# Second layer: output projection, norm before the experts and router logits in one program, tile by tile

## The reference, cut to what matters

```python
def finish(o):                                  # inside diff_mixer
    o = rms_norm(o, p['subln'], SUBLN_EPS) * (1.0 - lambda_init)   # per head of 128 columns
    return o.reshape(*o.shape[:2], C_HEADS * 2 * HEAD_DIM) @ p['w_out']
...
x = x + mods_l[2] * out_l
hl = modulate(rms_norm(x), mods_l[3], mods_l[4])        # x * rstd * (1 + scale) + shift
...
grp_logits = hf @ w_grp.astype(f32) + b_grp.astype(f32)         # moe_ffn, 4 groups
exp_logits = (hf @ w_rt.astype(f32) + b_rt.astype(f32)).reshape(n, N_GROUPS, EXPERTS_PER_GROUP)
```

## Time and profile before

| what | us |
|---|---|
| median of three runs | 4664.04 |
| span of the profiled execution | 4663.1 |
| first DMA of the output projection to its first product | 3585.46 to 3631.87 |
| products of the output projection to the last one | to 3762.4 |
| rest of that phase, and the norm | to 3812.1 |
| the router's logits | to 3833.1 |
| the rest of the routing | to 3890.5 |
| experts and most of the combination | to 4640 |

### The profile page before, as it was taken

How to read it: one execution, slowest core, us unless ns; L and a number is a source line. 1 busy time by engine, 2 the same in 40 slices (tenths; PEclk the granted TensorE clock), 3 DMA queues, 4 the chain that set the end, 5 groups by cost and what they waited for, 6 DMA issues and landing times. The chain is left out here.

```text
span 4663.1 us, 88181 instructions
## 1 busy us (share of the span) xinstructions
PE 3727.8 (80%) x34186; PEld 2390.1 (51%) x34187; DVE 1882.9 (40%) x4414; ACT 1372.4 (29%) x3096; POOL 592.2 (13%) x926
## 2 busy tenths in 40 slices
PE   4998995698898685599999539989996654999973
PEld 1886553688888673133333128876664531333321
DVE  3322555677777563300000264327775332000004
ACT  2212664366664212011111021116665120111111
POOL 0000000144444220200000202100000102000001
PEclk7999997899999897699999759989998867999986
DMA  7221001122222245968899852240001234589995
GB/s 301 76 84 69 10 10 47 42 72 74 78 69 77 83 149 197 302 253 309 307 389 392 333 195 93 77 157 11 11 10 64 79 115 190 199 323 369 407 427 218
DMA packets 254657, 777.07 MB, mean 167 GB/s; under 512 B 77972, under 2 KB 166568, under 8 KB 223624
## 3 DMA queue, kind: packets, MB, share of 16 engines
q1 hardware_dynamic: 201064, 641.55, 36.9%
q10 hardware_dynamic: 38736, 82.33, 4.6%
q0 software_dynamic: 14544, 48.79, 2.7%
HBM read 647.12 MB, written 117.60 MB: 164 GB/s over the span
## 5 line engine op out<-in xcount | busy, mean ns | idle before, releaser
L3076 PE MATMUL ex_bY<-ex_w,ex_aT 128*64 x880 | 389.1, 595 | 73.5 <-DVE ex_aT L3139 73.5
L3076 PE MATMUL ex_bG<-ex_w,ex_xT 128*64 x880 | 403.9, 614 | 39.6 <-SPq L2997 25.8
L3079 PE MATMUL ex_bG<-ex_w,ex_xT 128*64 128x512 f32 x880 | 403.9, 614 | 0.0
L3079 PE MATMUL ex_bY<-ex_w,ex_aT 128*64 128x512 f32 x880 | 389.4, 595 | 0.0
L3076 PE MATMUL ex_bU<-ex_w,ex_xT 128*64 x880 | 386.6, 592 | 0.0
L3079 PE MATMUL ex_bU<-ex_w,ex_xT 128*64 128x512 f32 x880 | 386.6, 592 | 0.0
L3137 DVE TENSOR_TENSOR ex_a<-ex_sg,ex_bU 128x512 f32<-128x512 f32 x55 | 37.9, 689 | 812.4 <-PE ex_bU L3079 812.4
L3076 PEld LDWEIGHTS ex_bG<-ex_w,ex_xT 128*64 128x64 f32 x880 | 123.8, 142 | 301.7 <-issue 301.7
L3076 PEld LDWEIGHTS ex_bY<-ex_w,ex_aT 128*64 128x64 f32 x880 | 116.0, 137 | 299.7 <-issue 299.7
L1036 DVE TENSOR_SCALAR_CACHE_REDUCE ad_p<-ad_S 128x512 f32<-128x512 f32 (+1 forms) x384 | 215.7, 600 | 101.5 <-PE ad_S L946 101.5
L3076 PEld LDWEIGHTS ex_bU<-ex_w,ex_xT 128*64 128x64 f32 x880 | 120.6, 137 | 247.4 <-issue 247.4
(11 more groups left out here) (450 smaller groups left out, 8544.0 us busy)
## 6 DMA issues: line engine op xcount, KB each, us to landing
ex_w<-in_moe_w_gate SPq DMA_DIRECT2D x64, 2048.0 KB, 11.9
ex_w<-in_moe_w_up SPq DMA_DIRECT2D x64, 2048.0 KB, 16.2
ex_w<-in_moe_w_down SPq DMA_DIRECT2D x64, 2048.0 KB, 15.3
yb_dram<-ex_y ACTq DMA_DIRECT2D x55, 512.0 KB
rt_mw<-in_mod_w SPq DMA_DIRECT2D x24, 1024.0 KB, 7.6
n_mw<-in_mod_w SPq DMA_DIRECT2D x16, 1024.0 KB, 8.2
kb_dram<-rs_pout SPq DMA_DIRECT2D x60, 256.0 KB, 2.8
rs_KB<-kb_dram SPq DMA_DIRECT2D x120, 128.0 KB, 2.6
```

The costliest lines, as they stand in the source:

```text
L3076: nc.tensor.matmul(bank[0:BR, :], stationary[:, k, 0:BR], w[:, ds(slot0 + (offset + k * n), 512)], start=k == 0, stop=k == tiles - 1)
L3079: m = nc.tensor.matmul(bank[BR:P, :], stationary[:, k, BR:P], w[:, at:at + 512], start=k == 0, stop=k == tiles - 1)
```

## The change

`odd_outproj_phase` takes the place of `outproj_phase` and of the second layer's `norm_phase`, and it makes the logits too. `outproj_phase` and its loop over pairs are gone; the new streams are written out for 8 tiles.

- The inner norm's factor times (1 - lambda_init) is now a column of 128 values, one for each row of a weight strip. ACT and DVE put it into the weights while they split them (L2741, L2794). POOL's multiplication of `o` is gone.
- Four buffers for weight strips, and separate buffers `sq` for the squares. PE's first block of products takes strip k as soon as it is split (`w_rest`, k + 1). Only one gate row is loaded.
- A class `RowNorm` holds the next norm and the logits of a tile: ACT squares and takes the root, DVE scales, POOL adds the shift row, SP stores `h`, PE turns the tile through one bank, ACT copies it, PE multiplies (the turned rows stationary, the 36 router columns moving) and DVE adds the bias into `L`, which stays in SBUF. PE does this for tile q - 2 while it makes the products of tile q.
- `route_phase` with `L` given loads neither weights nor biases and begins with the choice of the group.

In the diff, the four loops inside `odd_outproj_phase` are those of SP, PE, ACT and DVE, in this order; the last two stand behind the split of the weights.

```diff
-def outproj_phase(nc, sems, tag, d, layer, o_dram, w_dram, src, dst, first=0, subln=None):
+class RowNorm:
...
+    def load(self, sp, cond):
...
+        for t, which in ((self.shift_row, SHIFT2), (self.scale_row, SCALE2)):
+            sp.dma_start(t[:, :], row_of(d["mods"][l, cond, which * D:(which + 1) * D])).then_inc(self.const_in, 16)
...
+    def prepare(self, dve):
+        self.nc.vector.memset(self.eps[:, :], RMS_EPS).then_inc(self.eps_set, 1)
+        dve.wait_ge(self.const_in, 16 * 6)
+        self.nc.vector.tensor_scalar(self.scale_row[:, :], self.scale_row[:, :], 1.0, None, ALU.add).then_inc(self.ready, 1)
...
+    def shift(self, pool, q):
...
+        self.scaled.wait(pool, q)
+        self.shifted.did(self.nc.gpsimd.tensor_tensor(self.h[:, u, :], self.h[:, u, :], self.shift_row[:, :], ALU.add))
...
+    def turn(self, pe, q, b):
+        u = q % 2
+        if b == 0:
+            self.shifted.wait(pe, q)
+        if q or b:
+            self.lifted.wait(pe, q if b else q - 1, 0 if b else 1)
+        for k in range(4):
+            z = self.nc.tensor.transpose(self.bankH[:, k * P:(k + 1) * P], self.h[:, u, (4 * b + k) * P:(4 * b + k + 1) * P], self.ident[:, :])
...
+    def logits(self, pe, q):
...
+        self.lifted.wait(pe, q)
+        if q:
+            self.taken.wait(pe, q - 1)
+        for k in range(KT):
+            z = self.nc.tensor.matmul(self.bankL[:, 0:TD], self.hT[:, u, k, :], self.wr[:, k, :], start=k == 0, stop=k == KT - 1)
...
+def odd_outproj_phase(nc, sems, d, o_dram, src, dst, h_dram, L):
...
+                for q in range(T):
+                    if q + 4 < T:
+                        load_o(q + 4)
+                    store_x(q)
+                    if q + 2 < T:
+                        load_x(q + 2)
+                    norm.store(sp, q, row(q))
...
+                turn(0)
+                turn(1)
+                for q in range(T + 2):
                     for b in US:
+                        if q < T:
+                            products(q, b)
+                        if q >= 2:
+                            norm.turn(pe, q - 2, b)
+                    if q + 2 < T:
+                        turn(q + 2)
+                    if q >= 2:
+                        norm.logits(pe, q - 2)
...
+                for q in range(T + 2):
+                    if q >= 2:
+                        for b in US:
+                            norm.lift(act, q - 2, b)
+                    if q + 2 < T:
+                        lead(q + 2)
+                    if q + 3 < T:
+                        square(q + 3)
+                    if q < T:
+                        norm.square(act, q)
+                        norm.root(act, q)
+                    if q + 3 < T:
+                        root(q + 3)
...
+                norm.prepare(dve)
+                total(2)
+                unit(2)
+                for q in range(T + 2):
+                    if q < T:
+                        result(q)
+                    if q + 2 < T:
+                        rest(q + 2)
+                    if q + 3 < T:
+                        total(q + 3)
+                    if q < T:
+                        norm.scale(dve, q)
+                    if q >= 2:
+                        norm.take(dve, q - 2)
+                    if q + 3 < T:
+                        unit(q + 3)
...
-def route_phase(nc, sems, tag, d, layer, hT, first, slot_dram, slots, gates, tok, table, sil=None):
+def route_phase(nc, sems, tag, d, layer, hT, first, slot_dram, slots, gates, tok, table, sil=None, L=None):
...
-    outproj_phase(nc, sems, "o1", d, 1, o, d["od_w_out"][0], x2, x3, CT, d["od_subln"][0])
-    moe(1, x3, out, CT, d["final_gain"])
+    with ExitStack() as ctx:
+        L = static(ctx, "L1", [P, NT - CT, TD])
+        odd_outproj_phase(nc, sems, d, o, x2, x3, h, L)
+        moe(1, x3, out, CT, d["final_gain"], L=L)
```

More of the change, by code:

```diff
@@ L2517, in outproj_phase @@
-        rounds = (NT - first) // 2
+        row = lambda q: (CT + q) * P
         with nc.Block() as block:
@@ L2570, in _, with turn @@
+            @block.gpsimd
+            def _(pool):
+                for q in range(T):
+                    norm.shift(pool, q)
             @block.tensor
             def _(pe):
-                pe.wait_ge(c_in, 16 * nc_in)
-                def turn(m, u):
-                    if pre:
-                        po.wait(pe, f"sub{u}", m)
-                    else:
-                        pe.wait_ge(o_in[u], 16 * m + 16)
+                pe.wait_ge(ident_in, 16)
+                def turn(q):
+                    normed.wait(pe, q)
@@ L2600, in body @@
[L2600 to L2616 removed]
+                            z = nc.tensor.transpose(tr[b][:, k * P:(k + 1) * P], o[:, q % 2, (4 * b + k) * P:(4 * b + k + 1) * P], ident[:, :])
@@ new lines, in turn, with products @@
+                        turned.did(z)
+                def products(q, b):
+                    u = q % 2
+                    if b == 0:
+                        rested.wait(pe, q)
+                    if q >= 2:
+                        gated.wait(pe, q - 2, b)
+                    for k in range(KT):
+                        if q == 0 and b == 0:
+                            pe.wait_ge(w_rest, k + 1)
+                        for n, (p, r) in enumerate(((oh, wh), (oh, wl), (ol, wh))):
+                            z = nc.tensor.matmul(acc[u][b][:, :], p[:, u, k, :], r[:, k, b * 512:(b + 1) * 512], start=k == 0 and n == 0, stop=k == KT - 1 and n == 2)
+                    multiplied.did(z)
@@ L2644, in _, with square, root @@
-                pair_loop(act, first, body)
+                act.wait_ge(eps_set, 1)
+                def square(q):
+                    act.wait_ge(o_in[q % 2], 16 * (q // 2 + 1))
+                    if q >= 2:
+                        summed.wait(act, q - 2)
+                    squared.did(nc.scalar.activation(sq[:, q % 2, :], o[:, q % 2, :], ACT.Square))
+                def root(q):
+                    summed.wait(act, q)
+                    if q >= 2:
+                        inverted.wait(act, q - 2)
+                    rooted.did(nc.scalar.activation(sd[:, q % 2, :], ss[:, q % 2, :], ACT.Sqrt, scale=1.0 / P, bias=eps[:, 0:1]))
@@ new lines, in result @@
+                def result(q):
+                    u = q % 2
+                    if q == 0:
+                        dve.wait_ge(gate_in, 16)
+                    for b in US:
+                        multiplied.wait(dve, q, b)
+                        gated.did(nc.vector.tensor_tensor(t[:, u, b * 512:(b + 1) * 512], acc[u][b][:, :], gate[:, b * 512:(b + 1) * 512], ALU.mult))
+                    dve.wait_ge(x_in[u], 16 * (q // 2 + 1))
+                    for b in US:
+                        gated.wait(dve, q, b)
+                        x_done.did(nc.vector.tensor_tensor(x[:, u, b * 512:(b + 1) * 512], t[:, u, b * 512:(b + 1) * 512], x[:, u, b * 512:(b + 1) * 512], ALU.add))
```

372 lines of the change are left out of this document (207 added, 165 removed).

## The result

| | before | changed |
|---|---|---|
| median, first comparison | 4666.09 us (4 runs) | 4584.07 us (4 runs, 4582.33 to 4590.16) |
| ratio, 95% interval | | 0.9823 [0.9811, 0.9834] |
| median, second comparison | 4671.97 us (9 runs) | 4589.61 us (5 runs, 4578.53 to 4591.02) |
| ratio, 95% interval | | 0.9819 [0.9805, 0.9832] |
| span of the profiled execution | 4663.1 | 4580.5 |

The change saves 82 us of the whole. The forecast was 4567 with a range from 4554 to 4598: the mechanism held, and the gain was put 17 us too high. 8.3 us of these lie in the forecast stretch (150.8 forecast, 159.1 measured). 6.0 us lie in code that is the same in both kernels: the first load of `o` stands 4.5 us later than in the trace of before (3590.00 against 3585.46), and the part behind the stretch is 1.5 us longer.

The account below looks back on a forecast made before the run. TensorE was taken as idle in a 247.7 us stretch, waiting for strips, GpSimd's multiplication and the norm. Last product 130.5 + tail 14.3 + phase end 0.9 + constants 5.1 = 150.8, 96.9 less: 4567 us, range 4554 to 4598.

Parts of the forecast that it names:

- likeliest case: Whole kernel: the forecast mechanism without the rivals, 4557 to 4581 us, chance 0.70.
- first block done: Start: TensorE's first block follows the strip splits and ends 25.5 us behind the first load, ends 21 and 33.
- wait ahead of tile 2: Turn of tile 2: TensorE waits 2.0 us for constants and the tile's norm, ends 0 and 6.
- products and all between them: Tile loop: 15 product blocks 81.8, low clock 1.6, turned tiles 5.4, transposes 5.0, logits 5.0, seams 4.2 us.
- tail, last product to last bias: Behind the last product: tile 7's result, norm, shift, transposes, logits and bias, 14.3 us, ends 12 and 17.
- phase end: Between the last bias and the routing phase: 0.9 us.
- routing's constants: Start of routing: wait for six constants whose landing was hidden before, 5.1 us, with ScalarE's table load fitting inside.
- first rival: Start held by loads at 250 GB/s: tile 2's wait grows to 8 us, 10 us more, 4577; chance 0.14.
- Cover of the norm: Tile loop: next norm hidden between products with 5 us of cover, 3 us if VectorE and GpSimd lock each other.
- second rival: Tile loop: VectorE and ScalarE set the pace, 17 us a tile instead of 14.3, 19 more, 4586; chance 0.12.
- third rival: Tile loop: each block waits for its own tile's chain, 36.8 us a tile, 61 slower, 4725; chance 0.02.
- fourth: Experts: changed rounding moves tokens and the block count, about 27 us a block either way; chance 0.02.

Follow-up runs that it names:

- e1: Changed kernel with loads of o tiles 2 and 3 ahead of the small rows, VectorE waiting for constants only before its first scaling: stage 151.4 us, whole 4578.45 us.
- e7: Changed kernel with only 4 of the 8 pieces of each logit sum multiplied: stage 152.1 us, whole 4582.85 us.
- e5: Changed kernel with the shift row added by VectorE instead of GpSimd: stage 160.9 us, whole 4583.00 us.
- e9: Changed kernel with unread 512-column filler products on TensorE behind the last output product: stage 157.5 us, whole 4578.95 us.
- e8: Changed kernel with the six routing constants loaded while the tiles run: stage 154.9 us, whole 4580.69 us.
- e6: Changed kernel with the first product waiting for all eight strips of the first weight block: stage 157.5 us, whole 4584.01 us.
- e10: Changed kernel with the edits of e1, e5, e8 and e9 together: stage 144.5 us, whole 4571.03 us.
- e11: Changed kernel with the edits of e1 and e8 together: stage 144.5 us, whole 4572.77 us.

## Why the prediction was right, and where it was off

The sign, the size within 17 us, and the mechanism are as predicted; but the median of 4584.07 lies above the 4557 to 4581 that the forecast held for its likeliest case, in the part of the range that was there for the first two rivals, and neither of them came as it was described. Two of the signs named beforehand failed: the pause ahead of tile 2 is not under 6 us, and the tail is 17 us, not 14. The signs of the mechanism held: 247.7 us became 159.1, TensorE's waits per pair are gone, norm and logits lie between the products, and the experts' stretch is what it was. Step by step, measured against the forecast:

| step | forecast | measured | difference |
|---|---|---|---|
| first block done | 25.5 | 23.5 | -2.0 |
| wait ahead of tile 2 | 2.0 | 9.1 | +7.1 |
| products and all between them | 103.0 | 104.5 | +1.5 |
| tail, last product to last bias | 14.3 | 17.1 | +2.8 |
| phase end | 0.9 | 1.0 | +0.1 |
| routing's constants | 5.1 | 3.9 | -1.2 |
| stage | 150.8 | 159.1 | +8.3 |

- **Start.** Right, even a little short: the last strip's split ended at 22.8 us, forecast 24.2. The loads did not hold VectorE's splits up here, though in some of the runs one landed 2 us late.
- **The wait ahead of tile 2** is the term that failed, and outside its own ends of 0 and 6. Of the 7.1 us, 3.3 only show that TensorE was there at 29.3 instead of 32.6; the turn itself comes at 38.4 where the forecast had 34.6. (Its own terms gave 27.0 for the constants, not 28, and a wait of 0.7; the 2.0 was taken above them.) The step said "the small router weights, 1 us": they were counted by their bytes. By bytes the count came true: the queue was worked off at about 28.5 us. But SP had stood 4.97 and 3.26 us in the issues of the router's weights and a bias row; the last bias row was issued at 28.9 and was in at 32.6, and "tile 2, which is loaded right behind" was issued at 29.3 and landed at 34.2. e1 took the wait away and was left with 151.4. That this is nearly the forecast's number is partly chance: its last result is 1 us early, its tail 3 us long, its constants 1 us short. The first rival had named this place and a wait of 8 us, but its reason, a low rate of the loads, is not what the profile shows: the window in which SP issued the router's weights moved 385 GB/s. The bytes moved, the issues were slow.

```profile
3612.00:3616.00 4.00, 3.55 (x16) 2.58 (x15) 0.80 (x2) 0.00 (x0) 0.00 (x0) 1.00 1.02 385
```

- **Products.** Pace 14.6 us against 14.3. Two errors met: the logits are 1.79 us instead of 1.0, since the trace has two instructions for each of these float32 products and only one for each transpose, which was taken as the nearest row (an instruction takes 0.11 us in both); and the seam of 0.6 us taken from layer 0 does not exist here. e7 showed that this time is on the path.
- **Cover of the norm.** Right. VectorE's product stretched from 1.22 to 3.30 us beside GpSimd; in layer 0, with half the columns, it was from 0.66 to at most 1.77, and the sum had left 2.4 us for it. The Trainium skill says (SBUF — State Buffer, section SBUF: two separate sides) that of two such instructions the one that starts first holds a shared port pair to its end and the other is blocked. The trace agrees closely: the product ended at 3663.75, 1.1 us behind GpSimd's end at 3662.67, as if it had begun about there. It stayed in its cover: TensorE wanted that tile 5.5 us later, at 3669.24. e5 confirmed both. The second rival falls.
- **Tail.** 17.1 instead of 14.3, just above its upper end of 17. The working followed tile 7 alone. It left out that the logits of tile 6 stand ahead of tile 7's turn: 2.1 us of wait for TensorE. The logits at half clock, put at 2.2 with their wait, are 3.63 and 0.69. e9 showed that at least 3.1 us are the clock's, with the fillers' own time already paid.
- **Constants.** Right in kind, and e8 showed them to be a wait of 4 us that hides ScalarE's table load, too. The last constant is issued 2.3 us behind the first and is in 1.6 us later; the forecast had 2.6 and 2.5.
- **Outside the stage.** 4.5 us in front and 1.5 behind are in no step. In front, thirteen executions spread over 12 us; the trace of before is a single one, 1 us ahead of the earliest of them. Scatter can explain the 4.5 us, but it isn't shown that it explains all: both comparisons of medians give 82 us, the stretch alone 88.6. Where the scatter arises was not traced.

The third rival (lock step, slower) did not come: in six tiles TensorE waited for no tile. Neither did the fourth: the page after counts 55 blocks again.

## What to carry to other kernels

A small DMA behind large ones can cost the time that it holds the issuing engine, and not the time of its bytes: read the durations of the issues on SP's own timeline. Put whatever is urgent ahead of it, and don't let an engine wait for it earlier than it needs the data. Small work can go between another tile's products at nearly its own TensorE time (2.8 instead of 8.8 us a tile here), but at the end of the loop it stood alone here, at half clock, and there every engine's queue order counts, not only the last tile's chain. And where a start gains nothing, look for the wait behind it that takes the gain up: e6 took 6 us of it away and lost nothing.

## What the hardware showed that was not expected

- SP needs 4.97 us (4.68 to 5.69 in twelve executions) to issue the load of the router's weights and 3.26 (to 3.70) for a bias row when loads of 0.5 MB are queued ahead; 0.58 and 0.43 us at the start of the old routing phase, with no such load ahead.
- Eight float32 products with 36 moving columns are 16 instructions: 1.79 us at full clock, 3.6 at half. With half as many a tile was 0.9 us shorter, so it is not a fixed cost.
- A wait of 2.31 us for the last strip was followed by a stretch of 4 us at a granted clock of 0.73 (e10), one of 2.12 us by one at 0.75 (e1); behind one of 0.96 us there (e11) and one of 2.14 us ahead of tile 2's turn (e6) it stayed at 1.00. The length of the wait alone doesn't decide it. In the tail the products of 128 and 36 columns with gaps of 0.69 us let it fall, and 512 columns put into the same gaps held it at 1.00.
- With GpSimd and VectorE at once one of them is held: VectorE 3.30 us beside GpSimd's 2.39 where it began 0.17 us later; and the one time that VectorE began first (3635.06, 1.22 us, against 3635.07), GpSimd took 3.48.
